# Mean squares of the second layer's head norms: one float32 matmul, or two on a rounded part and a remainder

## The reference, cut to what matters

```
def _rmsnorm(x, g):
    y = xf * rsqrt(mean(xf * xf, axis=-1) + NORM_EPS)      # over the 128 numbers of one head
    return y * g
q  = _rope(_rmsnorm(q, q_norm_g), cos, sin)                 # 16 heads
k  = _rope(_rmsnorm(k, k_norm_g), cos, sin)                 # 4 heads
ki = _rope(_rmsnorm(ki, ik_norm_g), cos_i, sin_i)           # 1 head, for the indexer
...
score = sum over heads of relu(qi . ki) * wi ; sel = top_k(score, 64)
p = softmax(q . k[sel]) ; o = p @ v[sel] ; out = o @ w_o
```

## Time and profile before

| | us |
|---|---|
| median of 3 runs | 2233.77 (2232.78 to 2234.11) |
| profiled execution | 2232.74 |
| its span, first to last instruction | 2230.9 |
| PE busy | 2220.7 |
| DVE busy | 1495.7 |
| ACT busy | 1165.7 |
| POOL busy | 2.5 |

### The profile page before, as it was taken

The page is one execution under the profiler, slowest core; times in us unless marked ns, Lnnn a source line. Parts: engine busy times, 40 slices in busy tenths (PEclk is TensorE's granted clock), DMA queues, the critical chain, the costliest instruction groups (busy, mean ns, idle before and its releaser), DMA issues. The chain is left out here.

```text
span 2230.9 us, 35512 instructions
## 1 busy us (share of the span) xinstructions
PE 2220.7 (100%) x12842; PEld 1956.3 (88%) x12842; DVE 1495.7 (67%) x1772; ACT 1165.7 (52%) x1394; POOL 2.5 (0%) x9
## 2 busy tenths in 40 slices
PE   9999999999999999999999999999999999999999
PEld 8888898888888888888889888888888888888888
DVE  7666556677777777555578887677777777774444
ACT  7555555555555555444455456555555555553332
POOL 0000000000000000000000000000000000000000
PEclk9999999999999999999999999999999999999999
DMA  7555545555555556555565544455555555556554
GB/s 268 162 169 175 172 161 180 194 184 191 185 197 179 197 179 199 191 191 191 190 204 199 179 151 131 152 180 189 190 194 187 187 191 191 185 193 203 198 194 136
DMA packets 113543, 412.05 MB, mean 185 GB/s; under 512 B 12736, under 2 KB 13376, under 8 KB 113472
## 3 DMA queue, kind: packets, MB, share of 16 engines
q1 hardware_dynamic: 112464, 407.49, 55.3%
q10 hardware_dynamic: 576, 1.97, 0.2%
q0 software_dynamic: 432, 1.57, 0.2%
HBM read 408.88 MB, written 2.10 MB: 184 GB/s over the span
## 5 line engine op out<-in xcount | busy, mean ns | idle before, releaser
L667 DVE TENSOR_TENSOR w_lo<-raw,w_hi 128x1024 fp32r<-128x1024 f32 x772 | 938.1, 1223 | 679.8 <-ACT w_hi L263 674.2
L1191 PE MATMUL psum<-xg,w_hi 128*128 128x512 f32 (+1 forms) x3936 | 1360.0, 391 | 2.5 <-DVE xg L682 2.5
L263 ACT CAST w_hi<-raw 128x1024 fp32r<-128x1024 f32 x772 | 804.4, 1049 | 781.5 <-PE psum L1191 778.2
L1191 PE MATMUL psum<-xg,w_lo 128*128 128x256 f32 (+1 forms) x3936 | 1093.9, 278 | 0.0
L1191 PEld LDWEIGHTS psum<-xg,w_hi 128*128 128x128 f32 x3936 | 736.8, 187 | 158.4 <-issue 2.2
L1191 PEld LDWEIGHTS psum<-xg,w_lo 128*128 128x128 f32 x3936 | 744.0, 189 | 2.5 <-issue 2.2
L1191 PE MATMUL psum<-hid,w_hi 128*128 128x512 f32 x1408 | 488.2, 391 | 0.0
L1191 PE MATMUL psum<-hid,w_lo 128*128 128x256 f32 x1408 | 394.2, 280 | 0.0
L1191 PEld LDWEIGHTS psum<-hid,w_hi 128*128 128x128 f32 x1408 | 263.3, 187 | 57.7
L1191 PEld LDWEIGHTS psum<-hid,w_lo 128*128 128x128 f32 x1408 | 266.1, 189 | 0.0
L1191 PE MATMUL psum<-att,w_hi 128*128 128x512 f32 x512 | 178.7, 393 | 0.1
(11 more groups left out here) (152 smaller groups left out, 891.8 us busy)
## 6 DMA issues: line engine op xcount, KB each, us to landing
raw<-w_all SPq DMA_DIRECT2D x772, 512.0 KB, 3.4
xres<-x_in SPq DMA_DIRECT2D x4, 512.0 KB, 7.2
cst<-consts_in ACTq DMA_DIRECT2D x2, 768.0 KB, 5.7
out_t<-xres POOLq DMA_DIRECT2D x3, 512.0 KB, 4.1
out_t<-xres SPq DMA_DIRECT2D x4, 128.0 KB, 1.8
vecs<-vecs_in ACTq DMA_DIRECT2D x1, 354.0 KB, 6.4
avg_d<-consts_in SPq DMA_DIRECT2D x1, 64.0 KB, 9.3
vecs<-vecs_in ACTq DMA_DIRECT2D x1, 32.0 KB, 4.2
```

The source lines that it names most:

```text
L263: act.copy(w_hi[:, c % RING, :], raw[:, c % RING, :]).then_inc(hi_ready, 1)
L667: dve.tensor_tensor(w_lo[:, c % RING, :], raw[:, c % RING, :], f32(w_hi[:, c % RING, :]), ALU.subtract).then_inc(lo_ready, 1)
L1191: return pe.matmul(o, lhsT, rhs, start=start, stop=True, skip_group_check=True)
```

## The change

The squares go into `rsn` in float32. ACT copies them from there to `usq[:, 0]`, rounded; DVE subtracts that from the squares into `usq[:, 1]` (`squares_low`). PE takes two matmuls into the same place, each with a rounded copy `avg_r` of the averaging matrix, in the place of one float32 matmul with `avg_h`. `squares_low` stands in slot 0 of the next block on DVE, behind that slot's split (for norm 0 in slot 2 of the pieces of ki and wi; for norm 10 in slot 0 of the output projection). PE now waits for `usq_ready` where it waited for `rb_sq`.

```
-        usq = sb("usq", [P, 2, T], F32, l1)
+        usq = sb("usq", [P, 2, 2, T], F32R, l1)
+        avg_r = sb("avg_r", [P, P], F32R, l1)
 ...
                 if nb is not None:                       # ACT, evac
                     act.wait_ge(rb_u, nb + 1)
-                    act.activation(usq[:, 0:nh, :], tu[:, 0:nh, :], ACT.Square).then_inc(rb_sq, 1)
+                    if not (isinstance(nb, int) and nb == 0):
+                        act.wait_ge(ms_ready, nb)
+                    act.activation(rsn[:, 0:nh, :], tu[:, 0:nh, :], ACT.Square).then_inc(rb_sq, 1)
+                    act.wait_ge(rb_sq, nb + 1)
+                    act.copy(usq[:, 0, 0:nh, :], rsn[:, 0:nh, :]).then_inc(usq_hi, 1)
 ...
                     act.wait_ge(cst_in, 32)
+                    act.copy(avg_r[:, :], avg_h)
                     act.copy(idr[:, :], ident).then_inc(id_ready, 1)
 ...
+            def squares_low(nh, nb):                     # DVE
+                dve.wait_ge(usq_hi, nb + 1)
+                dve.tensor_tensor(usq[:, 1, 0:nh, :], rsn[:, 0:nh, :], f32(usq[:, 0, 0:nh, :]), ALU.subtract).then_inc(usq_ready, 1)
 ...
+                if e == 2:                               # DVE, pieces of ki and wi, behind the split
+                    squares_low(1, 0)
 ...
                     split(base + e + RING, i, per)       # DVE, block1
+                    if e == 0 and prev is not None and prev[0] in ("k", "q"):
+                        squares_low(2, prev[1])
 ...
             def l1_tail(e):                              # DVE
+                if e == 0:
+                    squares_low(2, 10)
 ...
             def mean_squares(nh, nb):                    # PE
-                pe.wait_ge(rb_sq, nb + 1)
-                if not (isinstance(nb, int) and nb == 0):
+                pe.wait_ge(usq_ready, nb + 1)
+                if isinstance(nb, int) and nb == 0:
+                    pe.wait_ge(id_ready, 2)
+                else:
                     pe.wait_ge(rsn_ready, nb)
-                mm(psum[:, 5, 0:nh * T], avg_h, usq[:, 0:nh, :], True).then_inc(ms_ready, 1)
+                mm(psum[:, 5, 0:nh * T], avg_r[:, :], usq[:, 0, 0:nh, :], True)
+                mm(psum[:, 5, 0:nh * T], avg_r[:, :], usq[:, 1, 0:nh, :]).then_inc(ms_ready, 1)
```

More of the change, by code:

```diff
@@ L190, in build @@
         rb_copied, rb_sum, rb_u, rb_sq = sem("rb_copied"), sem("rb_sum"), sem("rb_u"), sem("rb_sq")
+        usq_hi, usq_ready = sem("usq_hi"), sem("usq_ready")
         ms_ready, ln_ready, rsn_ready = sem("ms_ready"), sem("ln_ready"), sem("rsn_ready")
```

## The result

| | before | after |
|---|---|---|
| median, us | 2233.94 (2232.78 to 2234.16, 4 runs) | 2277.63 (2276.68 to 2280.55, 4 runs) |
| ratio | | 1.02, 95% interval 1.0187 to 1.0213 |
| profiled execution, us | 2232.74 | 2278.41 |
| span, us | 2230.9 | 2276.6 |
| mean granted TensorE clock | 1.000 | 0.992 |

The change made the kernel 43.7 us slower; 29.5 were forecast, and 2277.63 lies outside the range of 2256 to 2274.

A forecast was written before the change was run, and what follows sets the result against it. PE was taken to bound the kernel. Late-subtraction waits net of PE's savings, 17.7 + 2.1 + 5.6 + 2.6 + 0.8 + 0.7 = 29.5 us, on the kernel before gave 2263 us, range 2256 to 2274.

The forecast's parts named there:

- The late subtraction: Subtraction queued in DVE's next slot 0: low squares at s (PE's end of the block before) + 12.33, PE waits 3.93 us.
- some 25 us in eleven waits: Sign expected in the profile after: PE's total wait at the matmul on avg_r, six waits near 3.9 us.
- Paid anew in each block: Query blocks: the chain restarts from the later s, so the stall recurs; net 3.54 us each for norms 5 to 9.
- The cast's 0.64 in front of the output rounding: On ACT, the added cast delays whatever follows the square, including out_hi, by 0.64 us.
- PE's price of the pair, 0.46: Mean square on PE: two rounded matmuls take 0.46 us against 0.86 for the float32 one, saving 0.39 each.
- The sum without the clock, 2263.3: Whole kernel: waits less PE's savings add 29.5 us, giving 2263.3 us at an unchanged clock.
- Forecast as worked out, clock unchanged: Case 1, whole kernel: PE waits at the mean squares without its clock falling; 2263 us, chance 0.68.
- Case 2: PE's stalls also lower its clock, 2.2 us per stall; 2265 (one) to 2276 us (six), chance 0.16.
- Work taken from PE is worth its full length: PE, busy for all but 10 of 2230.9 us: removed work counts in full, 4.0 us if all is hidden.
- Rival 4: Low squares come in time and PE keeps its 4.0 us; 2229.7 us, chance 0.07 with all mixtures below 2238.
- DVE's idle time: Query block: DVE's 3.4 us idle are turns between engines in a dependent chain, not slack for the 0.69 us subtraction.

The follow-up runs named there:

- e5: Kernel of e1 with the subtractions of norms 5, 7 and 9 put back into slot 0 of the next block; 2256.71 us.
- e7: Against the kernel before: norms 4 to 10 split, ACT rounds the output ahead of the square, DVE subtracts between maxes and normalise; 2229.01 us.
- e8: Kernel before with only ACT's order changed, output rounded ahead of the square, float32 mean squares kept; 2231.41 us.
- e4: Changed kernel plus eight or twelve filler matmuls on PE ahead of each wait for the subtraction; 2263.75 us.
- e9: As e7, but ACT keeps the old order of square and output rounding, with the cast behind both; 2233.67 us.
- e1: Changed kernel with DVE's subtraction moved up, directly behind the scaling in the same slot; 2242.77 us.
- e2: Kernel before plus the change's cast and subtraction into an unread buffer, float32 matmul kept, PE not waiting for them; 2245.26 us.

## Why the prediction was wrong

Its direction, place and mechanism held; the size did not, by the term of the clock.

- **The late subtraction.** Low squares at s + 12.33, measured s + 12.38. The waits of norms 5 to 9 were to be 3.93; they are 3.84, 3.92, 3.74, 3.82 and 3.84. Norm 10: 3.58, measured 3.52. Norm 4: 2.5, measured 2.86. Norm 1: 2.4, measured 2.24. The eight waits forecast one by one came out within 0.4, 27.8 us in all for 28.1. The "some 25 us in eleven waits" of the signs is less than this list of the forecast's own adds up to; all eleven take 33.9, with 2.36 and 3.35 at norms 2 and 3.
- **Paid anew in each block.** Held, by the waits themselves and by e5.
- **The cast's 0.64 in front of the output rounding.** Held: 1.20 from square to rounding for 0.54.
- **PE's price of the pair, 0.46.** Held: e7's period is 0.36 below e8's, for the 0.39 worked out.
- **The sum without the clock, 2263.3.** e4, the same kernel with the clock held up, takes 2263.75. That the two agree to 0.5 us is partly luck: from trace to trace e4 is 31.2 us longer than before (spans 2262.1 and 2230.9) for the 29.5, with a period of 19.4 for 19.2, and the rest vanishes because before's traced execution was 1.2 below its median.
- **The step that failed: "Forecast as worked out, clock unchanged", with 0.68.** Case 2, the clock, is what happened, and it had 0.16. The sum held nothing for the clock, though the waits that it forecast were three times the longest in the rows; the runs showed 13.9 us for it (changed kernel against e4). Case 2 itself had the price of a spell too high (2.2; 13.9 us over nine spells are 1.5 each, and block by block the changed kernel's periods are 1.4 to 1.6 us longer than e4's, but 2.7 at norm 6), the number too low: six waits of 3.6 to 3.9 us were taken to be at risk, and the waits of 2.24, 2.86 and 3.35 us lowered the clock too. The two errors nearly cancel: case 2's 2276 is 1.6 below the measured time. The range should have reached it; with the trace's start showing the lower level after idleness, a gap three times the longest seen deserved more than one chance in six. The rule of the Trainium skill (TensorE: Matmul & The Clock Gate, "HAM oscillation — how this bites in real kernels"), that gaps between bursts can put the array back to half clock in every pass of a loop, agrees with this trace at nine of ten waits.
- **"Work taken from PE is worth its full length".** Wrong in the query blocks as long as nothing waits. (Behind a late mean square it is PE that the others wait for, ACT 1.73 us at 1349.71, and there the sum's 0.39 per norm is to be had.) e9 shows it: with the work hidden, PE's 2.7 us are not to be had, because DVE's round is as long. Rival 4's 2229.7 was not reached by moving the work alone, in the two places tried; e1 is at 2242.8 and e9 at 2233.7. It took a shorter DVE round as well (e7).
- **DVE's idle time.** The forecast said that the 3.4 us were turns inside a chain, and that held: e2's work, which the busy shares would have hidden, costs 11.3 us. What the forecast did not draw from it is that this chain closes on itself in 15.6 us, so that DVE bounds a block as much as PE does.

What stays open: why a wait of one length lowers the clock in one place and not in another. In the traced executions 2.31 (e1), 2.36 (changed kernel) and 2.71 us (e2) left it at 1.00, while 2.24 and 2.30 did not. It may differ between executions of one kernel: nine spells took the mean granted clock of the changed kernel down by 0.008, so the 0.999 of four executions of e1 and two of e2 would fit one spell each, but no trace of these was kept.

## What to carry to other kernels

When an operand is prepared on another engine, ask behind what the preparation is queued and when the consumer arrives, both counted from the same event; a slot's name says nothing about time, since here the helpers' slot 0 ends after PE's slot 1. An engine that is 78% busy may still have a round (the time from an instruction to the same one in the next pass) as long as the bound engine's: add up its chain of turns, idle times included, before calling added work free or a saving on the bound engine a gain. And price each new gap on TensorE twice, once as the wait and once for the matmuls at the lower clock behind it.

## What the runs showed of the hardware that was not expected

A wait on PE as short as 2.24 us was followed by matmuls at the 1.2 GHz level (granted clock 0.60 over the next 4 us), while one of 2.36 us in the same execution was followed by 1.00, and so was one of 2.71 us in e2. With the subtraction early, a wait of 2.31 us left the clock at 1.00; with three late, the wait of 2.30 us at the same norm lowered it:

```profile
1297.50:1301.50 4.00, 3.99 (x22) 3.48 (x23) 3.76 (x5) 2.73 (x5) 0.00 (x0) 1.00 0.33 112
```

```profile
1296.90:1300.90 4.00, 4.00 (x13) 3.39 (x14) 3.78 (x5) 2.43 (x4) 0.00 (x0) 0.57 0.34 114
```

So from 2.2 to 2.7 us it went either way, once for the same wait in nearly the same program; every wait of 2.86 us and more in these traces was followed by the lower level. And matmuls that compute nothing, put into the gaps, bought 13.9 us.
